# One attention turn per pair of heads instead of per batch in three mixers of a four-layer transformer step

## The reference

```
q, k, v = split(h @ w_qkv)              # 16 query heads of 64; 4 key heads (A, B) or 16 (D)
q, k = rms_norm(q), rms_norm(k)         # per head; in A and B then rotated for latent tokens
context rows:  p = softmax(q k^T / 8 [, sink])   over the 128 context keys;   o = p v
latent rows:   p = softmax(q k^T / 8 [+ mask or bias] [, sink])
               over 256 latent keys and 128 cached keys together;             o = p v
x = x + gate * (o @ w_o)
```

## Time and profile before

| | |
|---|---|
| median of 3 executions | 2922.31 us (2921.38 to 2922.79) |
| the profiled execution's own time | 2923.23 us |
| its span, first to last instruction | 2921.4 us |
| PE busy | 2892.8 us (99%) |
| PE weight loads | 2808.3 us (96%) |
| DVE busy | 2275.1 us (78%) |
| ACT busy | 1253.1 us (43%) |
| POOL busy | 161.1 us (6%) |
| mean granted TensorE clock | 0.999 of full |
| chain that ended last | PE 57%, issue 38%, DVE 3%, ACT 1%, DMA 1% |

### The profile page before, as it was taken

How to read it: one execution, slowest core, us unless ns; L and a number is a source line. 1 busy time by engine, 2 the same in 40 slices (tenths; PEclk the granted TensorE clock), 3 DMA queues, 4 the chain that set the end, 5 groups by cost and what they waited for, 6 DMA issues and landing times.

```text
span 2921.4 us, 44432 instructions
## 1 busy us (share of the span) xinstructions
PE 2892.8 (99%) x17597; PEld 2808.3 (96%) x17597; DVE 2275.1 (78%) x3460; ACT 1253.1 (43%) x2009; POOL 161.1 (6%) x171
## 2 busy tenths in 40 slices
PE   8999999999999999999999999999999999999999
PEld 6999979999999998999999998899999999989999
DVE  6889987888787887888788777778888887777653
ACT  3332564433333266443333348644333334664432
POOL 0000220000000030000000012000000001320000
PEclk9999999999999999999999999999999999999999
DMA  7555414555455512455455531255555555324342
GB/s 289 208 210 215 153 46 166 193 196 207 180 190 191 218 63 93 180 194 212 179 191 199 198 121 46 75 199 194 200 194 190 194 207 196 109 75 175 127 145 92
DMA packets 87723, 490.22 MB, mean 168 GB/s; under 512 B 11825, under 2 KB 13169, under 8 KB 51377
## 3 DMA queue, kind: packets, MB, share of 16 engines
q1 hardware_dynamic: 83696, 480.42, 44.6%
q0 software_dynamic: 3904, 8.24, 1.1%
HBM read 485.33 MB, written 3.29 MB: 167 GB/s over the span
## 4 chain that ended last, share of the span: by engine, by line
PE 57%; issue 38%; DVE 3%; ACT 1%; DMA 1%; POOL 0%; SPq 0%; DVEq 0%; POOLq 0%; ACTq 0%
PE ps L858 16%; PE ps L877 8%; PE ps L863 8%; PE ps L910 5%; PE ps L1105 4%; PE ps L881 4%; PE ps L842 1%; PE ps L1040 1%; PE ps L1189 1%; PE ps L1080 1%; DMA boot<-in_mod_w 1%; PE ps L1021 1%; PE ps L1025 1%; PE ps L947 0%; PE ps L1125 0%
## 5 line engine op out<-in xcount | busy, mean ns | idle before, releaser
L858 PE MATMUL ps<-h_hi,w_hi 128*128 128x386 f32 x2688 | 908.1, 338 | 0.0
L858 PE MATMUL ps<-h_lo,w_hi 128*128 128x386 f32 x2688 | 893.3, 332 | 0.0
L1667 DVE TENSOR_TENSOR w_lo<-w_raw,w_hi 128x2048 fp32r<-128x2048 f32 (+3 forms) x281 | 703.2, 2502 | 30.0 <-ACT w_hi L1317 29.7
L1694 DVE CUSTOM_DVE_ANT_0 F_junk<-F_slab,cond,mod_b 128x1024 f32<-128x1024 f32 x544 | 706.9, 1299 | 13.1 <-DVE mod L1694 0.5
L1317 ACT ACTIVATE w_hi<-w_raw 128x2048 fp32r<-128x2048 f32 (+3 forms) x274 | 568.3, 2074 | 15.1 <-DMA w_raw<-in_ffn_dn 11.2
L858 PEld LDWEIGHTS ps<-h_lo,w_hi 128*128 128x128 f32 x2688 | 512.5, 191 | 0.0
L858 PEld LDWEIGHTS ps<-h_hi,w_hi 128*128 128x128 f32 x2688 | 503.0, 187 | 0.0
L863 PE MATMUL ps<-h_hi,w_lo 128*128 128x386 f32 x2688 | 494.3, 335 | 0.0
L877 PE MATMUL ps<-F_act_hi,w_hi 128*128 128x384 f32 x1408 | 473.6, 336 | 0.0
L877 PE MATMUL ps<-F_act_lo,w_hi 128*128 128x384 f32 x1408 | 473.3, 336 | 0.0
L863 PEld LDWEIGHTS ps<-h_hi,w_lo 128*128 128x128 f32 x2688 | 468.9, 187 | 0.0
(11 more groups left out here) (397 smaller groups left out, 3511.5 us busy)
## 6 DMA issues: line engine op xcount, KB each, us to landing
w_raw<-in_ffn_gu SPq DMA_DIRECT2D x176, 1024.0 KB, 4.8
F_slab<-in_mod_w SPq DMA_DIRECT2D x272, 512.0 KB, 5.6
w_raw<-in_ffn_dn SPq DMA_DIRECT2D x64, 1408.0 KB, 6.4
w_raw<-in_d_w SPq DMA_DIRECT2D x8, 1536.0 KB, 6.7
boot<-in_mod_w SPq DMA_DIRECT2D x8, 1024.0 KB, 10.2
w_raw<-in_a_w SPq DMA_DIRECT2D x4, 1536.0 KB, 6.7
w_raw<-in_b_w SPq DMA_DIRECT2D x4, 1536.0 KB, 6.7
w_raw<-in_c_w SPq DMA_DIRECT2D x8, 544.0 KB, 3.6
```

Of the source, the lines that this page charges most:

```text
L858: pe.matmul(ps[:, 2 * par + u, 0:N_MOVE], w[0][:, k, u, :], h[:, k, :], start=(k == 0 and h is h_hi), stop=False)
L1667: dve.tensor_tensor(w_lo[par][:, 0:w], w_raw[par][:, 0:w], w_hi[par][:, 0:w], ALU.subtract).then_inc(w_split_lo.sem, 1)
L1694: dve.tensor_tensor_reduce(out=junk[:], in0=w, in1=cond[:, c, :], scale=scale, scalar=mod_b[:, n:n + 1], op0=ALU.mult, op1=ALU.add, accum_ ...
```

## The change

In A, B and D the loop over batches becomes a loop over pairs, `for pair in range(PAIRS + 1)`; C keeps its loop. On PE a turn is: scores of both batches of the pair, `turn_p` of the previous pair's first batch, filling pieces, `turn_p` of its second batch, filling pieces, `turn_qk` of the next pair, filling pieces, `values` of both batches of the previous pair. The amount of work is the same, but for the `hold_clock` of mixer A, which goes. On ACT `p_copy` of the second batch comes in different places: before the exponentials where the turn has no projection pieces, between the two batches' exponentials in odd turns of A and B with pieces, after both otherwise. On DVE both maxima come first, then both inverses; `head_sums` stands ahead of the maxima, and `rotate_heads`, `head_bias` and the low split behind the inverses.

```diff
--- before.py
+++ after.py
@@ -187,6 +187,32 @@
     if b in drain:
         return drain[b]
     return (table.get(b, []), []) if b % 2 == 0 else ([], table.get(b, []))
+
+
+def pair_fills(kind, p):
+
+
+
+    g = p if kind == "D" else p // 2
+    if p >= PAIRS or g + 2 >= GROUPS[kind]:
+        return [], [], []
+    if kind == "D":
+        return [(g + 2, 0, 0, KD)], [(g + 2, 1, 0, KD)], [(g + 2, 2, 0, KD)]
+    if p % 2 == 0:
+        return [(g + 2, 0, 0, KD)], [(g + 2, 1, 0, 2)], [(g + 2, 1, 2, 4)]
+    return [(g + 2, 1, 4, KD)], [(g + 2, 2, 0, 4)], [(g + 2, 2, 4, KD)]
+
+
+def pair_ahead(kind, p):
+
+
+    if p == PAIRS:
+        return [(0, 5), (1, 0), (1, 1)], [(1, 2), (1, 3)], [(1, 4), (1, 5), (0, 6), (1, 6), (2, 0)]
+    if kind == "D":
+        table = {6: ([(0, 0), (0, 1)], [(0, 2)], []), 7: ([(0, 3)], [(0, 4)], [])}
+    else:
+        table = {4: ([(0, 0), (0, 1)], [], []), 5: ([(0, 2)], [], []), 6: ([(0, 3)], [], []), 7: ([(0, 4)], [], [])}
+    return table.get(p, ([], [], []))
 
 
 def wo_bank(m):
@@ -1260,14 +1286,38 @@
                 if kind != "C":
                     projection(s, 1, TT - 1, KD - 2, KD)
                 pe.wait_ge(mixer_in, n_loads[kind])
-                for b in range(BATCHES + 3):
+                for pair in range(PAIRS + 1 if kind != "C" else 0):
+                    fill, early = pair_fills(kind, pair), pair_ahead(kind, pair)
+                    if pair < PAIRS:
+                        scores(s, 2 * pair)
+                        scores(s, 2 * pair + 1)
+                    if pair >= 1:
+                        turn_p(s, 2 * pair - 2)
+                    for piece in fill[0]:
+                        projection(s, *piece)
+                    for m, p in early[0]:
+                        output(s, m, p)
+                    if pair >= 1:
+                        turn_p(s, 2 * pair - 1)
+                    for piece in fill[1]:
+                        projection(s, *piece)
+                    for m, p in early[1]:
+                        output(s, m, p)
+                    if pair + 1 < PAIRS:
+                        turn_qk(s, pair + 1, "qk")
+                    for piece in fill[2]:
+                        projection(s, *piece)
+                    if pair >= 1:
+                        values(s, 2 * pair - 2, "cl")
+                        values(s, 2 * pair - 1, "cl")
+                    for m, p in early[2]:
+                        output(s, m, p)
+                for b in range(BATCHES + 3 if kind == "C" else 0):
                     first, last = ahead(kind, b)
                     if b < BATCHES:
                         scores(s, b)
                     for m, p in first:
                         output(s, m, p)
-                    if kind == "A" and b == BATCHES - 5:
-                        hold_clock(7, s, b - 2)
                     if 2 <= b < BATCHES + 2:
                         turn_p(s, b - 2)
                     for piece in fills(kind, b):
@@ -1291,7 +1341,9 @@
                             projection(s, *piece)
                     for m, p in last:
                         output(s, m, p)
-                begun = [[q for b in range(BATCHES + 3) for z in ahead(kind, b) for m, q in z if m == i] for i in range(KD)]
+                early = [ahead(kind, b) for b in range(BATCHES + 3)] if kind == "C" else [
+                    pair_ahead(kind, p) for p in range(PAIRS + 1)]
+                begun = [[q for y in early for z in y for m, q in z if m == i] for i in range(KD)]
                 for c in range(WO_STEPS):
                     n = n_down[kind] + n_g + c
                     par = n % 2
@@ -1604,7 +1656,47 @@
                 if kind == "C":
                     qk_copies(s, 0)
                 squares_of(s, 1)
-                for b in range(BATCHES + 3):
+                for pair in range(PAIRS + 1 if kind != "C" else 0):
+                    fill = [piece for part in pair_fills(kind, pair) for piece in part]
+                    done = [(g, t) for g, t, k0, k1 in fill if k1 == KD]
+                    if pair >= 2:
+                        o_hi(s, pair - 2)
+                    if pair >= 1:
+                        p_copy(s, 2 * pair - 2)
+                        if not fill:
+                            p_copy(s, 2 * pair - 1)
+                    if pair < PAIRS:
+                        context_probabilities(s, 2 * pair)
+                        latent_probabilities(s, 2 * pair)
+                        if kind != "D" and pair % 2 == 1 and done:
+                            raw(s, *done[0])
+                            done = done[1:]
+                            p_copy(s, 2 * pair - 1)
+                        context_probabilities(s, 2 * pair + 1)
+                        latent_probabilities(s, 2 * pair + 1)
+                    if done and (kind == "D" or pair % 2 == 0):
+                        raw(s, *done[0])
+                        done = done[1:]
+                        if pair >= 1:
+                            p_copy(s, 2 * pair - 1)
+                    if kind == "D":
+                        for g, t in done[0:1]:
+                            raw(s, g, t)
+                        done = done[1:]
+                    if pair + 1 < PAIRS:
+                        qk_copies(s, pair + 1)
+                    if fill and (kind == "D" or pair % 2 == 0):
+                        split_chunk(nd + (pair if kind == "D" else pair // 2) + 3)
+                    for g, t in done:
+                        raw(s, g, t)
+                    if fill and (kind == "D" or pair % 2 == 1):
+                        squares_of(s, (pair if kind == "D" else pair // 2) + 2)
+                    if pair >= PAIRS - 2 and pair < PAIRS:
+                        c = nd + n_g + 1
+                        split_hi_half(CB[s] + c - c % 2, c % 2, width(s, c), pair - (PAIRS - 2))
+                    if pair == PAIRS:
+                        o_hi(s, PAIRS - 1)
+                for b in range(BATCHES + 3 if kind == "C" else 0):
                     done = [[(g, t) for g, t, k0, k1, at_end in fills(kind, b) if k1 == KD and at_end == late]
                             for late in (False, True)]
                     if 2 <= b < BATCHES + 2 and not (per_pair(kind) == 1 and b == BATCHES - 3):
@@ -2156,7 +2248,33 @@
                         split_chunk(nd + 2)
                 if kind == "D":
                     head_bias(s, 0)
-                for b in range(BATCHES + 3):
+                for pair in range(PAIRS + 1 if kind != "C" else 0):
+                    g = pair if kind == "D" else pair // 2
+                    norm_next = g + 1 < n_g
+                    fill = pair_fills(kind, pair)[0]
+                    if pair >= 2:
+                        o_lo(s, pair - 2)
+                    if norm_next and (kind == "D" or pair % 2 == 0):
+                        head_sums(s, g + 1)
+                    if norm_next and kind != "D" and pair % 2 == 1:
+                        scale_heads(s, g + 1)
+                    if pair < PAIRS:
+                        maximum(s, 2 * pair)
+                        maximum(s, 2 * pair + 1)
+                        if norm_next and kind == "D":
+                            scale_heads(s, g + 1)
+                        inverse(s, 2 * pair)
+                        inverse(s, 2 * pair + 1)
+                    if norm_next and kind != "D" and pair % 2 == 0:
+                        rotate_heads(s, g + 1)
+                    if norm_next and kind == "D":
+                        head_bias(s, g + 1)
+                    if fill and (kind == "D" or pair % 2 == 1):
+                        split_chunk(nd + g + 3)
+                    if pair == PAIRS:
+                        split_chunk(nd + n_g + 1)
+                        o_lo(s, PAIRS - 1)
+                for b in range(BATCHES + 3 if kind == "C" else 0):
                     g, i = divmod(b, 2 * per)
                     norm_next = g + 1 < n_g
                     early = kind in "CD" and b % 2 == 0
```

## The result

The changed kernel takes **2934.78 us** (median of 6 executions, 2933.42 to 2938.10), the kernel before 2922.55 us (6 executions, 2921.36 to 2923.13): a ratio of 1.0046, with a 95% interval of 1.0035 to 1.0057. The forecast was 2936.0. The change makes the kernel slower, by some 12 us.

The account below looks back on a forecast made before the run. It took PE, busy 99% of the span, as the bound, with new waits outweighing some 17 us of saved steps: +10.3 us, plus 3.4 for two clock falls, made +13.7 and 2936.0 us. The range was 2908 to 2946.

Parts of the forecast that it names:

- Steps into and out of half-array operations: On PE in A, B and D: 0.15 to 0.2 us a step, 0.8 us a pair with projections, some 17 us saved.
- The waits beside projections: PE waits for ACT's `raw` and second `p_copy`; net A +2.8, B -0.6, D +1.9 us.
- The turns without projections: Scores wait for copies behind both exponentials, DVE's normalisation delays pair 5; net A +1.9, B +3.7, D +0.6 us.
- The clock: Granted clock falls to half behind PE's longest waits without projections; two falls at 1.7 us, +3.4 us.
- The waits don't come: Rival: ACT's copies are ready in time, so PE keeps its gain beside projections; 2910 us, chance 0.22.
- Gain and waits cancel: Rival: waits half as long as worked out and no clock fall, sum about -3 us; 2920 us, chance 0.15.
- The clock falls at most waits: Rival: ten clock falls, 17 us on top of 10.3, part of it hidden; 2946 us, chance 0.08.
- A's hold: Removing mixer A's seven idle matmuls, which fill a wait: costed at nothing, between 0 and 1.5 us gained.

Follow-up runs that it names:

- experiment 7: The changed kernel with idle matmuls in its waits: before the last pair's first transpose, the next query/key transposes and, in A and B, pair 6's scores; 2930.93 us.
- Experiment 6: Experiment 3's kernel with the two batches' values apart, before and behind the third filling piece, in turns with projection pieces; 2926.23 us.
- experiment 10: Experiment 9's kernel (pair turns only beside projections) with experiment 2's earlier raw copies; 2918.23 us, ratio 0.9985 to the kernel before.
- Experiment 1: The changed kernel with ACT's query and key copies between the two batches' exponentials in turns without projection pieces; 2931.02 us.
- experiment 8: Experiment 3's kernel without DVE's rotation of the last group's queries and keys in A and B, computation incomplete; 2919.93 us in one execution.
- Experiment 9: The changed kernel with pair turns only beside projections, and the kernel before's batch turns with A's hold elsewhere; 2924.61 us.
- experiment 4: The kernel before without the seven idle matmuls of mixer A's `hold_clock`; 2924.30 us.
- experiment 5: Experiment 3's kernel with idle matmuls in three waits of each of A, B and D; 2921.27 us.
- experiment 2: The changed kernel with earlier `raw` copies in turns with projection pieces, and the second `p_copy` earlier in odd turns of A and B; 2928.04 us.
- experiment 3: The changed kernel with both ACT order edits, of experiments 1 and 2, together; 2925.13 us.

## Why the prediction was right, point by point

The waits came where they were forecast and one fall of the clock more than forecast came with them; that the sum ended so near is in part luck. The table compares the two profiled executions.

| term | predicted | measured | of it a fall of the clock |
|---|---|---|---|
| A, with projections | +2.8 | +2.9 | |
| B, with projections | -0.6 | 0.0 | |
| D, with projections | +1.9 | +1.0 | |
| A, without | +1.9 | +1.9 | 1.6 |
| B, without | +3.7 | +4.7 | 1.6 |
| D, without | +0.6 | +1.9 | 1.6 |
| clock falls | +3.4 | in the three rows above | |
| mixer C | 0 | -1.7 | its fall did not come |
| sum | +13.7 | +10.7 | |

Without the clock, waits and steps made +7.6 us, not +10.3, since 1.6 us of A's measured +1.9 is a fall; three falls made +4.8, not +3.4; and C gave 1.7 back. The sum of 10.7 is 3.0 below the forecast's 13.7. Between the medians the difference is 12.2, and that these end only 1.2 us from the forecast (2934.78 against 2936.0) owes something to more falls than were counted on. The executions without any fall say the same: 2928.89 in experiment 7 and 2921.0 to 2922.1 before, some 7.5 us apart.

**Steps into and out of half-array operations: right in size.** I took 0.15 to 0.2 us a step and 0.8 a pair. Experiment 6 gives 0.17 a step. In D's turns of pairs 2 to 5 scores take 1.74 us instead of 1.94, values 1.68 instead of 1.84, 72 projection matmuls 13.04 instead of 13.17, but the transposes, which have two sides less, 2.33 instead of 2.28. These turns last 18.79 us in experiment 10, where PE's idle time is all but nil, and 19.22 before: 0.43 of 0.8. Most of what is missing is a small wait that PE's matmul rows don't show. It stands at the weight loads (PEld), in experiment 10's waits view for D:

```profile
PEld ps L941 <- ACT D_raw L1466: 1.0, 6, 0.2
```

and on the timeline of PEld and of ACT: the tile behind the six transposes starts 0.16 us late, since `raw` of the tile before lasts until 2536.93.

```profile
2536.06 0.76 PEld L1071 LDWEIGHTS ps<-ident,D_p 128*128 128x128 f32 x6
2536.98 0.19 PEld L941 LDWEIGHTS ps<-w_hi,h_hi 128*128 128x128 f32 x1 [0.16 <-ACT D_raw L1466]
```
```profile
2536.44 0.49 ACT L1466 ACTIVATE D_raw<-ps 128x384 f32<-128x384 f32 x1 [0.41 <-PE ps L941]
```

In pair 1, whose tiles start in another bank, the same six transposes take 0.57 us to the next matmul instead of 0.74. Two such waits a turn are 0.34 us, and 0.43 + 0.34 is the 0.8. Where two tiles share a bank, six transposes (0.57 us) are here too little to put between them, since the copy of 0.49 us starts only 0.2 us into them. I had costed only the wait for a late `raw`, not the one for a `raw` that comes at once.

**The waits beside projections: right in place, in D too long.** PE waits at L936 for `raw` and at L1012 for `p_copy`, 1.38 us in A's pair 1 (1.45 predicted). In D pairs 3 to 5 lose 0.95 us to waits (turns of 19.39 against 18.45, which is 18.79 less the two small waits), not 1.1 to 1.6; pair 2 took 19.58 instead of 20.05. In B pairs 1 and 3 took 12.69 and 13.02 instead of 12.3 and 12.85, so that its gain of 0.6 did not come.

**The turns without projections: right in mechanism, the sums too high.** Pair 4 takes 8.74 (9.05 predicted), pair 5 10.68 (11.35) and pair 6 8.28 without its fall (8.45) in A. The sum for a turn starts the exponentials at 4.6 us though it has the copies end at 4.7; that slip is small beside these differences. Experiment 1 shows that the order on ACT sets pairs 4 and 6, experiment 8 that DVE sets pair 5, as the forecast had it. Without falls the three stretches are 0.3, 3.1 and 0.3 us longer than before, where +1.9, +3.7 and +0.6 were predicted. Experiment 9 gives that back. What its stretches are shorter still than before, 0.9, 0.2 and 0.9 us, can be the 0.8 us of values that lie on the other side of the cut.

**The clock: right, and undercounted by one.** The forecast took two falls at 1.7 and named the waits of A's pair 5, D's pair 6 and B's pair 5. The clock fell behind these three, to 0.50 for 3.4 us, and a fall cost 1.6. Experiment 7 takes away the falls and leaves the waits: 3.9 us, with 2930.93 against the 2933 that the forecast gave for this case. Experiments 4 and 5 show 1.3 and 1.5 to 1.6 in other kernels. The Trainium skill, "TensorE: Matmul & The Clock Gate", section "HAM oscillation — how this bites in real kernels", says that idle gaps between bursts of matmuls throttle the array again. The trace agrees in A, B and D; in C, behind the same wait as before, it shows no fall, and in experiment 2 none came behind 3.3 us without work, so the rule says where one may come and not that it does. That the longest waits are the ones followed by a fall was therefore partly luck.

**The rivals.** "The waits don't come" falls with the idle time of 4.1, 1.2 and 2.4 us beside projections. Nor was its 2910 reached by taking away what could be taken: without most of the order's waits and without the falls (experiment 5) it is 2921.27. "Gain and waits cancel" is what experiment 3 shows for another order, not this one. "The clock falls at most waits" does not hold for the profiled execution, which has three falls, but comes nearer in others. The mean granted clock is 0.998 in the three fastest executions (2933.42 to 2934.11), 0.997 at 2935.45 and 0.996 at 2937.74 and 2938.10. A fall takes 0.0006 off the mean (3.4 us at half rate in 2932), so the two slowest had some six or seven falls, an estimate, and not ten. So two was too low for every one of the six.

What mattered less: taking A's hold away cost nothing by itself on PE, as costed, but before it kept a fall away from this pair (experiment 4), so up to 1.6 of the 12 us may be its; the fall in A now comes at another wait, and this share is argued, not shown. Whether the old seven matmuls in the old place would have kept the clock in the changed order was not tried; six and seven more in other places did.

## What to carry to other kernels

Merging small operations on half of the array saved 0.17 us here for each step into or out of them. It also doubles what the next engine does in one piece, and copies that release a bank should not stand behind that piece: moving them between or ahead of the two halves brought 7 us beside projections (experiment 2) and 10 in all (experiment 3), and keeping the finer turns where nothing fills the waits brought 10 by itself (experiment 9). A saving in a turn that another engine bounds is waited for there. And a wait of TensorE in a thinly filled stretch is to be counted twice, once as itself and once as a possible fall of the clock, which a few idle matmuls inside the wait avoided here.

## What the runs showed of the hardware beyond that

The same wait need not have the same effect on the clock. C's wait leaves PE busy for 1.71 of 3.40 us before, with a fall to 0.50 behind it, and for 1.70 of 3.40 us in the changed kernel, with the clock at 1.00. Nor does a long wait decide it: 3.3 us with PE busy for 0.02 us had no fall behind them in experiment 2, and the same wait had one in the changed kernel. The executions show the same scatter: those of the kernel before that ran beside the experiments lie at 2921.0 to 2922.1 with a mean granted clock of 1.000 or at 2922.6 to 2923.5 with 0.999, and of experiment 10's eleven three lie at 2916.6 to 2916.8 (1.000) and eight at 2918.0 to 2918.4 (0.999). A single profiled execution can so hide or show 1.7 us that aren't the change's. A fall can also move: in experiment 1 it left pair 6 of A and B and came in the turn after it, where the wait had stood before without one.

Nor need a fall cost anything. The profiled execution of the kernel before has a second one, from 35.84 to 39.25 us, which the changed kernel's lacks; mixer A's first scores start at 345.85 and 345.84 us all the same. What the program waited for there instead was not followed up.
